# A hybrid decoder step on one core: when the S5 parameters are transposed, and how tokens get to their experts

## What is computed

```python
def _s5(u, ...):                       # 32 groups of 64 states, 16 channels each
    dt = exp(log_step); mag = exp(lr * dt)
    ab_re, ab_im = mag * cos(li * dt), mag * sin(li * dt)
    f_re, f_im = (nr * lr + ni * li) / den, (ni * lr - nr * li) / den
    ...                                # scan h = ab * h + f * (B u);  y = C h + D u

def _hier_moe(h, w_rc, w_rf, w_eu, w_ed):
    g_sel = argmax(softmax(tok @ w_rc))            # one of 4 groups
    fine_sel = (tok @ w_rf)[group g_sel]           # its 8 experts
    top_w, top_i = top_k(softmax(fine_sel), 2)     # two of them
    ...                                            # weights normalized, times p_sel
    for each expert e: out += combine_w[:, e] * (silu(gate) * up) @ w_ed[e]

x = x + mixed                          # x1; mixed = (...) @ w_o
x = x + _hier_moe(_rmsnorm(x, norm_ffn_w), ...)
```

## Time and profile before

| | us |
|---|---|
| median of 3 runs | 1739.56 (1738.46 to 1739.89) |
| the profiled execution | 1737.92 |
| its span | 1736.2 |
| PE busy | 1519.3 |
| DVE, ACT, POOL busy | 700.4, 397.1, 222.0 |
| mean granted clock of PE | 0.941 of full speed |

### The profile page before, as it was taken

The page is one execution under the profiler, slowest core; times in us unless marked ns, Lnnn a source line. Parts: engine busy times, 40 slices in busy tenths (PEclk is TensorE's granted clock), DMA queues, the critical chain, the costliest instruction groups (busy, mean ns, idle before and its releaser), DMA issues. The chain is left out here.

```text
span 1736.2 us, 16020 instructions
## 1 busy us (share of the span) xinstructions
PE 1519.3 (88%) x6054; PEld 947.5 (55%) x6054; DVE 700.4 (40%) x1086; ACT 397.1 (23%) x639; POOL 222.0 (13%) x224
## 2 busy tenths in 40 slices
PE   8889999989998989699999599999807999999970
PEld 6556666645655656356989366555403444444430
DVE  4378676023243322885785333221241111111118
ACT  4111101015565563131211500011101111111113
POOL 0000010000000000254287000000041000000004
PEclk9998999999999999799899899999958999999995
DMA  5261148411100113324101722111127999999938
GB/s 160 72 101 49 50 131 240 116 50 40 38 27 26 38 26 89 92 62 139 57 1 29 298 75 75 62 60 64 43 73 302 377 367 373 370 368 367 368 144 292
DMA packets 191315, 247.83 MB, mean 143 GB/s; under 512 B 62548, under 2 KB 125432, under 8 KB 190976
## 3 DMA queue, kind: packets, MB, share of 16 engines
q1 hardware_dynamic: 165508, 186.79, 33.7%
q10 hardware_dynamic: 18140, 34.48, 5.1%
q0 software_dynamic: 7584, 25.44, 3.9%
HBM read 188.86 MB, written 57.82 MB: 142 GB/s over the span
## 5 line engine op out<-in xcount | busy, mean ns | idle before, releaser
L654 PE MATMUL P<-arena 128*128 128x352 f32 (+1 forms) x1728 | 547.0, 473 | 5.2 <-ACT arena L1791 5.2
L654 PEld LDWEIGHTS P<-arena 128*128 128x128 f32 (+1 forms) x1728 | 329.4, 194 | 193.1 <-issue 37.4
L1083 PE MATMUL P<-arena 128*128 128x512 f32 x512 | 227.8, 598 | 0.8 <-ACT arena L2060 0.8
L1083 PEld LDWEIGHTS P<-arena 128*128 128x128 f32 x512 | 95.8, 192 | 110.0 <-issue 110.0
L1031 PE MATMUL P<-arena 128*128 128x512 f32 (+1 forms) x288 | 126.8, 594 | 1.9 <-DVEq L1532 1.9
L999 PE MATMUL P<-arena 128*128 128x352 f32 x384 | 115.4, 464 | 10.1 <-DVE arena L1518 10.1
L1070 PE MATMUL P<-arena 128*128 128x512 f32 x256 | 115.3, 593 | 0.9 <-DVE arena L1661 0.9
L1641 DVE COPY arena<-P 128x512 f32<-128x512 f32 x32 | 22.1, 692 | 213.7 <-PE P L1057 213.7
L999 PEld LDWEIGHTS P<-arena 128*128 128x128 f32 x384 | 73.7, 192 | 52.0 <-issue 12.1
L1031 PEld LDWEIGHTS P<-arena 128*128 128x128 f32 (+1 forms) x288 | 50.9, 181 | 66.7 <-issue 64.2
L579 POOL TENSOR_TENSOR arena<-arena,N 64x256 f32<-64x256 f32 x96 | 80.0, 833 | 49.7 <-ACT arena L1994 26.9
(11 more groups left out here) (384 smaller groups left out, 1842.4 us busy)
## 6 DMA issues: line engine op xcount, KB each, us to landing
arena<-in_w_expert_up_dram SPq DMA_DIRECT2D x32, 2048.0 KB, 12.2
arena<-in_w_expert_down_dram SPq DMA_DIRECT2D x32, 1024.0 KB, 8.2
arena<-in_w_in_dram SPq DMA_DIRECT2D x36, 512.0 KB, 3.8
y_d<-arena ACTq DMA_DIRECT2D x32, 512.0 KB, 7.7
gate_d<-arena ACTq DMA_DIRECT2D x16, 528.0 KB, 4.1
arena<-gate_d SPq DMA_DIRECT2D x16, 528.0 KB, 4.5
arena<-in_x_prompt_dram SPq DMA_DIRECT2D x16, 512.0 KB, 4.3
y_d<-zero SPq DMA_DIRECT2D x1, 8192.0 KB, 33.2
```

What stands on the lines that cost most here:

```text
L654: m = pe.matmul(P[0:p, b + j, 0:TBK], w[:, k, 0:p], hT[:, k, TBK * j:TBK * j + TBK], start=f, stop=l)
L1083: m = pe.matmul(P[:, i % 2, :], xgT[i % 2][:, k, :], WU[i % NWE][:, k, :], start=k == 0, stop=k == KD - 1)
```

## The change

Four things. In job 1 PE transposes P7 at k = 3, the convolution state at k = 4 and the scan states at k = 6; the C matrices go to job 2, k = 1. ACT evicts u jobs 0 and 1 between its parameter copies, and jobs 2 and 3 behind them.

The routing is done for each token tile inside the output projection. Expert e has the fixed rows 128e to 128e + 127 of a new array x_d. PE transposes h2 of the tile one before, runs its router products, and sums the counts of the tile two before (`places`); DVE chooses and computes the places of each tile; POOL scatters the h2 rows themselves to x_d, two DMAs for a tile, leaving out rows beyond 128 of an expert. The first 32 expert tiles are then plain loads of x_d. Tokens beyond 128 of an expert go to further tiles by the old way (`further_rows`), only when there are any. The list's tables, the mixing weights and the rows of the result are computed by DVE in experts 1 to 4, and every engine waits for s_te and reads the number of tiles after expert 31. SP sends the weights of three experts when the last output matmul is done, behind its stores of h2.

The zeros of y_d are written in 8 parts behind the weights of jobs AB+1 to AB+8, and POOL, after its mask, waits for them and copies them twice (8 MB each) into x_d, so that its unused rows are zero.

The xr and h2 buffers move to another place of the arena, and SP's first loads of xr wait for s_mix. The diff, cut to its core:

```diff
+        x_d = dram("x_d", (E * 128, D))
...
+            run(0, E)
+            eng.wait_ge(s_te, 1)
             count = eng.value_load(te_i[0:1, NTILE:NTILE + 1], min_val=0, max_val=NTILE)
-            run(0, E)
...
-        EARLY = 1
+        Z_PARTS = 8
+        EARLY = NWE
...
+            pool.wait_ge(s_yz, 1 + 16 * Z_PARTS)
+            half = E * 128 // 2
+            for b in range(2):
+                pool.dma_start(x_d[half * b:half * b + half, :], y_d[128 * E:128 * E + half, :]).then_inc(s_sct, 16)
...
-            pool.wait_ge(s_zid, 16)
-            pool.wait_ge(s_pos, 1)
+            pool.wait_ge(s_sct, 32)
             for i in range(TT_):
                 n = rows(i)
+                pool.wait_ge(s_h2, i + 1)
+                pool.wait_ge(s_pos, i + 1)
                 for j in range(2):
-                    pool.indirect_dma_start(idx_d, bass.IndirectOffsetOnAxis(pos_i[0:n, j, i:i + 1], 0), tokf[0:n, i:i + 1],
-                                            None).then_inc(s_sct, 16)
+                    pool.indirect_dma_start(x_d, bass.IndirectOffsetOnAxis(pos_i[0:n, j, i:i + 1], 0), h2[i % 2][0:n, :],
+                                            None, bounds_check=E * 128 - 1, oob_is_err=False).then_inc(s_h2d[i % 2], 16)

             for b in range(2):
-                pool.wait_ge(s_h2d[b], 16 * ((TT_ + 1 - b) // 2))
-            pool.wait_ge(s_idx, 1)
+                pool.wait_ge(s_h2d[b], 32 * ((TT_ + 1 - b) // 2))
...
+                    if i < E:
+                        pool.dma_start(xg[i % 2], x_d[128 * i:128 * i + 128, :]).then_inc(s_xg[i % 2], 16)
...
+            def discretized():
                 pe.wait_ge(s_P7, 1)
...
+            def parameters(k):
+                if k == 3:
+                    discretized()
+                if k == 4:
+                    pe.wait_ge(s_par2, 16 * (11 + 2 * GA))
+                    bank = bank7()
+                    for f in range(12):
+                        m = pe.transpose(bank[:, 24 * f:24 * f + 24], CSTN[0:24, f, :], ident[0:24, 0:24])
+                    m.then_inc(s_7, 1)
+                if k == 6:
+                    bank = bank7()
+                    for d in range(2):
+                        m = pe.transpose(bank[:, 128 * d:128 * d + 128], STN[d], ident)
+                    m.then_inc(s_7, 1)
+
+            def output_rows(k):
+                if k == 1:
+                    bank = bank7()
+                    for q in range(4):
+                        m = pe.transpose(bank[:, 128 * q:128 * q + 128], CN[:, q // 2, q % 2, :], ident)
+                    m.then_inc(s_7, 1)
+
+            job(1, parameters)
+            job(2, output_rows)
...
+            def places(i):
+                pe.wait_ge(s_M, i + 1)
+                bank = bank6()
+                m = pe.matmul(bank[:, 0:E], later[:], Mt[:, i, :], start=True, stop=i == 0)
+                if i > 0:
+                    m = pe.matmul(bank[:, 0:E], ones[:], Pfx[:, i, :], start=False, stop=True)
+                if i == TT_ - 1:
+                    m = pe.matmul(bank[:, E:2 * E], ones[:], tot, start=True, stop=True)
+                m.then_inc(s_6, 1)
...
+                        if i >= 2 and (o, k) == (0, 3):
+                            places(i - 2)
+                        if i >= 1 and (o, k) == (0, 6):
+                            h2_transposed(i - 1)
+                        if i >= 1 and (o, k) == (1, 2):
+                            router(i - 1)
+            places(TT_ - 2)
+            h2_transposed(TT_ - 1)
+            router(TT_ - 1)
+            places(TT_ - 1)
...
+            def first_largest(o, v, top, scratch, highest, n):
+
+                link(dve.scalar_tensor_tensor(scratch, v, top, desf[:, 0:n], ALU.is_equal, ALU.mult))
+                link(dve.tensor_reduce(highest, scratch, AX, ALU.max))
+                link(dve.tensor_scalar(o, scratch, highest, None, ALU.is_equal))
+
+            def choose(i):
+                c = slice(i, i + 1)
+                group, chosen = ohg[:, i, :], sc32[:, 0, :].rearrange("p (g e) -> p g e", g=NG)
+                link(dve.tensor_reduce(m4[:, c], lg[:, i, :], AX, ALU.max))
+                first_largest(group, lg[:, i, :], m4[:, c], sc4[:, i, :], e2[:, c], NG)
+                link(dve.tensor_tensor(chosen, lf[:, i], group.unsqueeze(2).broadcast_to([128, NG, EG]), ALU.mult))
+                link(dve.tensor_reduce(fs[:, i, :], chosen.rearrange("p g e -> p e g"), AX, ALU.add))
+                link(dve.tensor_reduce(m8[0][:, c], fs[:, i, :], AX, ALU.max))
+                first_largest(oh8[0][:, i, :], fs[:, i, :], m8[0][:, c], sc8[:, i, :], e2[:, c], EG)
+                link(dve.scalar_tensor_tensor(fm[:, i, :], oh8[0][:, i, :], -1e30, fs[:, i, :], ALU.mult, ALU.add))
+                link(dve.tensor_reduce(m8[1][:, c], fm[:, i, :], AX, ALU.max))
+                first_largest(oh8[1][:, i, :], fm[:, i, :], m8[1][:, c], sc8[:, i, :], e2[:, c], EG)
+                for j in range(2):
+                    link(dve.tensor_tensor(E12[j][:, i], group.unsqueeze(2).broadcast_to([128, NG, EG]),
+                                           oh8[j][:, i, :].unsqueeze(1).broadcast_to([128, NG, EG]), ALU.mult))
+                link(dve.tensor_tensor(Mt[:, i, :], g(E12[0])[:, i, :], g(E12[1])[:, i, :], ALU.add))
+                if i == TT_ - 1:
+                    link(dve.memset(Mt[32:64, i, :], 0.0))
+                    link(dve.memset(Mt[64:128, i, :], 0.0))
+                upto = Pfx[:, i + 1, :] if i + 1 < TT_ else tot
+                dve.tensor_tensor(upto, Pfx[:, i, :], Mt[:, i, :], ALU.add).then_inc(s_M, 1)
+                dve.wait_ge(s_M, i + 1)
+
+            def places(i):
+                bk = bank6()
+                link(dve.tensor_scalar(sc32[:, 0, :], bk[:, 0:E], 128.0, SKIP, ALU.is_ge, ALU.mult))
+                ins = dve.tensor_tensor(slot[:, i, :], bk[:, 0:E], e_slot, ALU.add)
+                if i < TT_ - 1:
+                    read6(ins)
+                else:
+                    link(ins)
+                    read6(dve.tensor_copy(cnt, bk[:, E:2 * E]))
+                link(dve.tensor_tensor(slot[:, i, :], slot[:, i, :], sc32[:, 0, :], ALU.add))
+                for j in range(2):
+                    link(dve.tensor_tensor(sc32[:, j, :], slot[:, i, :], g(E12[j])[:, i, :], ALU.mult))
+                link(dve.tensor_reduce(pos[:, :, i], sc32[:, 0:2, :], AX, ALU.add))
+                dve.tensor_copy(pos_i[:, :, i], pos[:, :, i]).then_inc(s_pos, 1)
+                dve.wait_ge(s_pos, i + 1)
...
-                    router(i - 2)
+                    places(i - 2)
+                if i >= 1:
+                    router(i - 1)
+                    choose(i - 1)
...
             router(TT_ - 1)
+            choose(TT_ - 1)
+            places(TT_ - 1)
...
+                    if i == 1:
+                        mixing_weights()
+                        further_tiles()
+                    if i == 2:
+                        owners(0)
+                        owners(1)
+                        tile_table()
+                    if i in (3, 4):
+                        result_rows(i - 3)
+                    if i == 4:
+                        dve.sem_inc(s_te, 1)
...
+            u_job(0)
             read7(act.activation(conv_st
...
+            u_job(1)
             bk = bank7()
...
+            u_job(2)
+            u_job(3)
...
-                if i >= 2:
-                    h2_tile(i - 2)
+                if i >= 1:
+                    h2_tile(i - 1)
...
-            act.wait_ge(s_te, 1)
-            act.wait_ge(s_yz, 17)
+            act.wait_ge(s_yz, 1 + 16 * Z_PARTS)
...
-            tail = (NTILE - E) * D
-            sp.wait_ge(s_yz, 1)
-            sp.dma_start(y_d[128 * E:].rearrange("(p t) d -> p (t d)", p=128).rearrange("p (a b) -> p a b", b=128),
-                         zero[:].unsqueeze(1).broadcast_to([128, tail // 128, 128])).then_inc(s_yz, 16)
...
+                if AB < n <= AB + Z_PARTS:
+                    part = (NTILE - E) * 128 // Z_PARTS
+                    first = 128 * E + part * (n - AB - 1)
+                    sp.wait_ge(s_yz, 1)
+                    sp.dma_start(y_d[first:first + part].rearrange("(p t) d -> p (t d)", p=128).rearrange("p (a b) -> p a b", b=128),
+                                 zero[:].unsqueeze(1).broadcast_to([128, part * D // 128 // 128, 128])).then_inc(s_yz, 16)
...
-                e = sp.value_load(te_i[0:1, i:i + 1], min_val=0, max_val=E - 1)
+                e = i if i < E else sp.value_load(te_i[0:1, i:i + 1], min_val=0, max_val=E - 1)
...
-            sp.wait_ge(s_te, 1)
+            sp.wait_ge(s_wt, TT_)
             for i in range(EARLY):
                 expert(i)

-            sp.wait_ge(s_sct, 16 * 2 * TT_)
```

More of the change, by code:

```diff
@@ L241, in hybrid_step @@
         assert q + 18432 + 4 * NT <= ARENA
-        xr = [at(WR + i * D, D) for i in range(2)]
-        h2 = [at(WR + (2 + i) * D, D) for i in range(2)]
-        junk = at(WR + 4 * D, D)
         NWE = 3
```

(53 more changed lines are left out.)

179 lines of the change are left out of this document (74 added, 105 removed).

## The result

The changed kernel takes 1726.64 us (median of 4 runs, 1723.74 to 1730.11), beside 1739.01 for the kernel before on the same chip (1737.86 to 1739.89). The ratio is 0.993, with a 95% interval of 0.9919 to 0.9942. It is faster, by 12.4 us where 42.3 were forecast, and 1726.64 lies above the range. The profiled execution took 1730.11 us with a span of 1728.4; of before it was 1737.92 and 1736.2. It is the slowest of the four runs, so the timelines show a gain of 7.8 us where the medians show 12.4.

The account below looks back on a forecast made before the run. PE, busy for 88% of the span, was taken as the bound, through its waits. 14.8 + 29.5 - 1.0 - 1.0 = 42.3 us gave 1695.6 for the profiled run and 1697.3 us for the median, range 1688 to 1713.

Parts of the forecast that it names:

- What bounds the kernel: Whole kernel: PE is busy for 88% of the span, so gains come where PE waits.
- The three places that PE's waits named: Projection job 2's start (5.24 us wait), job 5 (5.55 us), and the stretch from output projection to first expert.
- Part 1: Parameter transposes and evictions in the projection jobs: two PE waits and slow restarts go, gain 14.8 us (10 to 16).
- Part 2: Zeros in eight parts, costed at nothing, and copy clearing x_d beside q, k, v jobs: 100 us long, price 1 us.
- second rival: q, k, v jobs: the copy into x_d doubles PE's waits for ACT, 11 us lost, 1708 us; chance 0.12.
- third rival: POOL's queue: the copy blocks POOL, which owes the decay mask from 687; at 60 GB/s 1787 us; chance 0.04.
- the 66 to 190 of the bounds: Copy into x_d: 66 us at the rate of the zeros, 190 us at that of a 512 KB gather.
- Part 3: Routing per tile in the output projection: first up-projection at 1283.7 against 1313.23, gain 29.5 us (16 to 32).
- The milder form of the first rival: Last two scatters: POOL's issues take 1.94 us beside DVE instead of 0.95, 2 us lost; chance 0.15 stated with first rival.
- The first rival: Output projection: DVE sets the pace, 1 to 2 us late in each of 8 tiles, 1705 to 1713 us; chance 0.15.
- Part 4: Tail after the experts: each engine reads the tile count there, loss 1.0 us (0.5 to 1.6).
- The chance of 0.62 for the whole sum: Whole kernel: the chance given to the forecast as it stands, 1690 to 1704 us.

Follow-up runs that it names:

- the copy in another place: Changed kernel with the two 8 MB copies into x_d issued only after the sixth block of the gated sum in the output stage: 1721.15 us, ratio 0.9899.
- The doubled copy: Changed kernel with the two copies made a second time, into a scratch array: 1774.39 us, ratio 1.0203.
- the run without the early weights: Changed kernel with the copies after the seventh eviction, and weights of experts 1 and 2 sent after the first two experts' rows landed: 1695.28 us, ratio 0.974.
- first part alone: Kernel before with only the moved parameter and output-row transposes and job 0 evicted ahead of the parameter copies: 1724.79 us, ratio 0.9914.
- clearing alone: Kernel before with only the zeros in 8 parts and the copy into x_d, which nobody reads: 1767.62 us, ratio 1.0156.
- the copy behind the store: Changed kernel with the copies waiting for the seventh eviction, behind ACT's second pair of stores to kk_d: 1701.83 us, ratio 0.9795.

## Why the prediction was wrong

**What bounds the kernel: right.** The three places that PE's waits named are where the gains came from.

**Part 1: right.** Forecast 14.8 us, 14.4 in the table and 14.4 in the run of this part alone. Job 2 starts without a wait, PE's transposes for DVE in job 5 run from 103.00 to 118.50 without one, where 5.55 us stood, and P7 was transposed at 49.10:

```profile
49.10 0.60 PE L724 MATMUL P<-shift_id,arena 16*128 16x16 f32 x7
...
103.00 0.60 PE L762 MATMUL P<-shift_id,arena 128*128 128x128 f32 x4
```

**Part 2: wrong, and this is the miss.** The step that failed is "Its price is what it takes from others meanwhile: 0 to 12 us (rival two), and I take 1". It measured 27.7 us in the trace and 28.5 by itself. The mechanism was written down as the second rival, with a chance of 0.12: small stores wait for the copy, and ACT is late. Its size was wrong. The rival doubled the waits that PE already had, 17.0 x 2/3 = 11 us. But a held issue doesn't scale with the waits of before. It lasts from the store to the end of the copy, 27.6 us, and nothing covers it: with the copy elsewhere PE already waits 2.93 us for VS at this place, with it 31.54. The rows for this sizing were there. SP's issue behind the zeros was held for 29.23 us of a transfer of 33.2; the prediction used that row for POOL in its third rival and not for the engine that has to compute after it issues. The right question was: who issues a DMA with many short runs while the copy is under way, and what does that engine owe next? Even that question misses the second price, the loads that land late (the copy in another place).

The duration of the copy was wrong as well, 53.4 us where 100 were taken, outside even the 66 to 190 of the bounds: 16.8 MB from 499.6 to 553.7 are 310 GB/s. That was to the good. The doubled copy, with its 102.7 us, gives an estimate of what the assumed duration would have cost: a hold near 77 us and 1774 us, the other side of the kernel before. No run has a single copy that slow. So it was luck that the loss stayed at 27.7 us: the prediction took a long copy as harmless at a duration at which it would have been worse.

**Part 3: right in mechanism, 3.7 us short.** Forecast 29.5 us net; measured 32.0 - 6.2 = 25.8. The output projection grew by 6.2 (forecast 5.4). From x1 of tile 8 to the first up-projection it was 32.85 us, where the steps of the sum give 1283.7 - 1253.8 = 29.9. Of the 3.0 us, 0.9 lie in DVE's chain up to the first of the last two scatters (16.8 us for 15.9), 1.1 in the landing of the scatter (4.5 where 3.4 were taken with POOL's step) and 1.1 between the first load and the up-projection (9.45 for 8.35). The last two are the crowding by 9 MB of weights, which the prediction named and sized at 1 us for the scatter and 1.5 for the load; the run without the early weights showed it to be 5.1 us in all. The milder form of the first rival, scatters that are issued at 1.94 us in place of 0.95, didn't come: the last two took 0.88 and 0.87.

The first rival, DVE as the pace of the output projection, didn't happen. x1 comes right behind the choice of the tile before, without idle time, but only 0.4 us later beside PE's last matmul than before (1.51 us from its start where it was 1.11). From x1 to x1 of full tiles it is 16.84 us (1201.56 to 1218.40) where it was 16.40 (1198.62 to 1215.02), which is the price of PE's own short products. The third rival didn't either: POOL issued the copies in 1.28 us and was never blocked.

**Part 4: open.** The tail grew by 3.4 us where 1.0 was taken. POOL's first gather comes 6.35 us after the last store in after and 6.68 in before, so the read of the count doesn't show in these two. The growth lies behind it, between the first gather and the end: 50.1 us for 46.4. But in the twelve profiled kernels, these two among them, this stretch took 45.9 to 50.1 us, and the two others whose tail is that of before took 47.9 (first part alone) and 47.1 (clearing alone). So the growth looks like scatter of the gathers; a run that shows it wasn't made. From the last store to the first gather it is 6.2 to 6.7 us in the three kernels with the old tail and 6.1 to 7.5 in the nine with the new one, on average 0.7 more. So the read may cost the 1 us that was forecast or nothing; one execution of each can't tell.

**The forecast without its error.** With the copy behind the store the kernel took 1701.8 us, and with the weights held back 1695.3. The forecast of 1697.3 lies between: it was a forecast for a kernel whose clearing is hidden. The range had a fault of its own. Its lower end of 1688 is not the sum of its bounds: the most that they give is 16 + 32 - 0.5 = 47.5 us, 1692. And the bad ends together, 10 + 16 - 12 - 1.6 = 12.4 us, give 1727, so the measured time lies where all parts would have gone badly, though two went nearly as forecast. The chance of 0.62 for the whole sum and the upper end of 1713 didn't allow for the one resource of which the prediction itself said that no row shows it.

## What to carry to other kernels

A transfer is not free because its own consumer is late: list the engines that issue DMAs while it runs, look for the one whose stores have many short runs and who has to compute next, and take as the price the time from that store to the end of the transfer, less that engine's slack. Look as well for the loads that an engine will wait for beside it: in the output stage one landed after 43.1 us in place of some 4.5. Then place the transfer behind such a store and away from such loads; one semaphore wait on the issuing queue was worth 25 us here, and holding back weights that are not wanted yet another 6.5. Shorter runs of the bulk copy shorten the hold only once they are short enough: 4 KB halved it, 16 KB did nothing.

## What the runs showed of the hardware

- The second part of a DRAM-to-DRAM copy of 16.8 MB in all landed 53.4 us after its issue in runs of 64 KB, 55.4 in runs of 16 KB and 55.7 in runs of 4 KB: the length of the run cost it nearly nothing.
- The copy, SP's weights and ACT's store moved the same number of packets side by side: 85, 86 and 85 in 18 us with packets of 64 KB, 512 bytes and 256 bytes.
- Two stores of 256 KB in runs of 256 bytes landed after a median of 31.6 us beside that copy, 25.9 beside the copy in 4 KB runs, and 81.2 beside the doubled one; with the copy elsewhere it was 3.3 us. These are the rows of DMA issues (queue, count, KB each, median us to landing) from 490 to 600 us, first of after and then of the kernel with the copy behind the store:

```profile
kk_d<-arena ACTq DMA_DIRECT2D x2, 256.0 KB, 31.6
```

```profile
kk_d<-arena ACTq DMA_DIRECT2D x4, 256.0 KB, 3.3
```

- The engine isn't held at the store itself (1.74 us for both) but at the next DMAs that it issues, here of 1.5 and 12 KB. In the timeline the held time stands beside these. It is the engine behind the store that is held; SP's issues beside the same copy took 0.37 us each, and its load landed after 36.0 us.
